# Zero matmuls in the places where TensorE is planned to stand

## The chip, the cores and the metric

The kernel runs on one core of a Trainium2 chip. The metric is device time in microseconds of one execution of the whole program; times are medians of several executions.

## What is computed

Two transformer-like blocks, one after the other, on a sequence of 256 tokens of width 2048, in float32. The first block has an "even" layer (a sparse attention with compressed, selected and windowed keys, called nsa; a differential attention; an attention to 256 memory rows) and an "odd" layer (an attention to the 64 best keys by an indexer, called dsa; memory attention again). The second block has two layers, each with four mixers side by side (retention, hgrn, mlstm, rwkv), an output projection, and a gated feed-forward net of width 5632.

```python
x = first_block(x, mem, ...)                 # even and odd layer
for l in range(DEPTH):                       # second_block, DEPTH = 2
    u = rms_norm_2(h, norm_pre_mix[l])
    p = (u @ w_in[l]).astype(jnp.float32)    # 2048 x 7952
    p_ret, p_hgrn, p_ml, p_rw = split_cols_2(p, GROUP_COLS)
    ...                                      # four mixers
    mixed = jnp.concatenate([o_ret, o_hgrn, o_ml, o_rw], axis=-1) @ w_out[l]
    h = h + rms_norm_2(mixed, norm_post_mix[l])
    u = rms_norm_2(h, norm_pre_ffn[l])
    ffn = (jax.nn.silu(u @ w_ffn_gate[l]) * (u @ w_ffn_up[l])) @ w_ffn_down[l]
    h = h + rms_norm_2(ffn, norm_post_ffn[l])
```

## The kernel before

Two kinds of work share TensorE. The **stream** is the projections. Their weights come in units of 256 rows by up to 512 columns. Each unit is split into a high part by ScalarE (line 514, two to four units ahead) and a low part by VectorE (line 527), and each product is three matmuls (high with high, low with high, high with low; line 621). A block of units is of kind `tokens` (two banks out of the first four, (0, 1) and (2, 3) in turn, moving rows of up to 512 weight columns), of kind `features` (up to four banks, 0 to 3 or 4 to 7, moving rows of 256 tokens), or of kind `plain` (line 600, f32). The activations that the stream multiplies have to be transposed first, by `turn` (line 738, transposes on line 745, then a high part by ScalarE and a low part by VectorE) or, at the first chunk after a norm, by `turn_first` (transposes on line 770).

The **lanes** are Python generators, one for each mixer or attention; they issue small f32 matmuls, transposes, and VectorE, ScalarE and GpSimd work in banks 4 to 7. A lane yields either nothing (due at once) or the semaphore marks that its next step will wait for.

The order of all engines' instructions is fixed when the program is built. Every engine has a planned clock (`pe.clock`, `dve.clock`, ...), every semaphore mark an expected time, and `expected_at` gives the latest of several. `weave` (line 434) picks the lane whose marks are due first, at time `at`, and asks `stream_first` (line 453) whether a chunk of the stream goes before it: it does when `at` is more than `SLACK` = 0.35 us behind the time at which the chunk can begin, when VectorE's or ScalarE's planned clock is 3.0 or 2.0 us ahead of it, or when TensorE's recent activity in the plan is below `ACTIVE`. Where no lane is due at all (`at` infinite: all wait for blocks of the stream), `fill(True)` transposes the next pieces and `step` runs a chunk. `fill` (line 545) waits for the finished mixer and calls `turn` itself. The planned cost of a VectorE operation is 0.16 us and 0.00104 us a column, whatever the operation (a reciprocal: six times as much a column).

A layer of the second block ends its output projection in `post_norm` (from line 1863 on): sums of squares by ScalarE (line 714, or 1825), a reduce and a power on VectorE and GpSimd (lines 723, 705, 706), then the update of the residual (line 1876), `turn_first`, and from there one `turn` after the other between chunks of the next projection.

Of the kernel before, what the change touches and what calls it, by code (L numbers as in the profile page):

```python
# [15 lines left out]
S = 256  # L16
# [4 lines left out]
UNIT = 2  # L21
# [4 lines left out]
DVE_LEAD, ACT_LEAD = 3.0, 2.0  # L26
PATIENCE = 0.1
WINDOW, ACTIVE = 3.4, 0.38
EPS = 1e-6
BIG = 1e30  # L30

# [99 lines left out]
def expected_at(marks):  # L131

    return max([expected.get((id(sem), value), 0.0) for sem, value in marks], default=0.0)
# [173 lines left out]
class Program:  # L307
# [3 lines left out]
    def build(self):  # L311
        nc = self.nc
        with ExitStack() as ctx:
            def sem(name):
                return ctx.enter_context(nc.semaphore(name))

            at = [(nc.sbuf_base + 31) // 32 * 32]
# [14 lines left out]
            self.low_split = Counter(sem("low_split"))  # L332
            self.unit_used = Counter(sem("unit_used"))
            self.bank_summed = Counter(sem("bank_summed"))
            self.first_loads = Counter(sem("ident_and_gains"), 16)
            self.mem_loaded = [Counter(sem(f"mem_loaded{i}"), 16) for i in range(4)]
            self.x_loaded = [Counter(sem(f"x_loaded{i}"), 16) for i in range(4)]
# [96 lines left out]
    def weave(self, *tasks):  # L434

        live = [[task, []] for task in tasks]
        while live:
            self.fill(False)
            self.lows()
            lane = min(live, key=lambda lane: self.due(lane[1]))  # L440
            at = self.due(lane[1])
            if at == math.inf:
                self.fill(True)
                assert self.step(), self.units[self.g][0].name
            elif self.stream_first(at):
                self.step()
            else:
                try:
                    lane[1] = next(lane[0])
                except StopIteration:  # L450
                    live.remove(lane)

    def stream_first(self, at):

        if self.g == len(self.units) or not self.can_run(*self.units[self.g]):
            return False
        blk, u = self.units[self.g]
        marks = [self.load_mark[self.g] if blk.kind == "plain" else self.low_mark[self.g]]
        if u + self.k == 0:
            marks += self.bank_free[blk.banks[self.n]]  # L460
        if blk.kind != "plain":
            marks += blk.AT.ready[blk.k0 + u * UNIT + self.k]
        begin = max(self.pe.clock, expected_at(marks))
        if begin < self.pe.clock + HOP and self.pe.activity() < ACTIVE:
            return True
        return (at > begin + SLACK or self.dve.clock > begin + DVE_LEAD or self.act.clock > begin + ACT_LEAD)
# [234 lines left out]

    def inv_rms(self, ss, n, eps=EPS):

        nc, dve, pool = self.nc, self.dve, self.pool
        pool.wait_ge(dve.did(nc.vector.tensor_scalar(ss, ss, 1.0 / n, eps, ALU.mult, ALU.add)))
        mark = pool.did(nc.gpsimd.tensor_tensor(ss, ss, self.minus_half[0:ss.shape[0], 0:ss.shape[1]], ALU.pow))  # L706
        dve.wait_ge(mark)
        return mark
# [305 lines left out]
    def first_turns(self):  # L1014

        nc, A, pe, act, dve, pool = self.nc, self.A, self.pe, self.act, self.dve, self.pool
# [52 lines left out]
        yield wanted  # L1069
        for q in (pe, act, dve):  # L1070
            q.wait_ge(*wanted, *[landed.now() for landed in self.x_loaded])
        for k in (1, 2):
            self.turn_rows(k, 4 + k)
            yield
# [1606 lines left out]
```

## Time and profile before

| | |
|---|---|
| time, median of 3 runs | 3916.73 us (3912.31 to 3918.07) |
| span of the profiled execution | 3913.3 us |
| TensorE busy | 3798.5 us (97%) |
| VectorE busy | 2256.0 us (58%) |
| ScalarE busy | 1795.6 us (46%) |
| mean granted clock of TensorE | 0.985 of full speed |
| chain that ended last | TensorE 88%, VectorE 6%, ScalarE 3% |

The span is from the first to the last instruction of one execution. TensorE is nearly always busy and nearly always at full clock, so what is left to see are the places where it stands or runs at the lower clock. In a timeline, a line gives the start, the duration of the merged instructions, engine, line of the kernel, operation, output and inputs, how many were merged, and in brackets how long the engine stood idle before them and who released it. An f32 matmul stands in the trace as two records, a fp32r matmul or a transpose as one.

### The profile page before, as it was taken

What the parts mean: (1) busy time and instruction counts of PE and PEld (TensorE: products, weight loads), DVE (VectorE), ACT (ScalarE), POOL (GpSimd) and SP (SyncE); (2) the same over time, 40 slices, a digit from 0 to 9 for tenths busy, and PEclk for the clock granted to TensorE, in tenths of its full rate; (3) what the DMA queues carried; (4) which work ended last, traced back from release to release, by engine and by line L of the source; (5) the groups of instructions that cost most, each with busy time, mean ns of one, the idle gap of its engine ahead of it and who ended that gap; (6) DMA issues with size and microseconds to landing.
All of it is one profiled execution on the core that took longest, in us unless ns stands there. A gap on an engine that the chain in (4) does not pass through costs nothing.

```text
span 3913.3 us, 49190 instructions
## 1 busy us (share of the span) xinstructions
PE 3798.5 (97%) x19948; PEld 3204.6 (82%) x19948; DVE 2256.0 (58%) x3532; ACT 1795.6 (46%) x2519; POOL 104.5 (3%) x61
## 2 busy tenths in 40 slices
PE   8999999999999999989999999999999989999998
PEld 7886778787898897778888888988987778888887
DVE  5665666675555746764454444566656664445444
ACT  6454545445454424544444444545325454444443
POOL 0000000000010000000000000010000000000000
PEclk9999999999999999999999999999999999999999
DMA  7655546563554405446666655544225446666654
GB/s 239 184 167 147 145 135 179 158 188 101 182 165 135 122 26 159 146 146 190 191 188 189 200 194 193 178 125 143 63 78 153 152 140 189 192 189 189 201 193 169
DMA packets 341426, 628.34 MB, mean 161 GB/s; under 512 B 21088, under 2 KB 63024, under 8 KB 340432
## 3 DMA queue, kind: packets, MB, share of 16 engines
q1 hardware_dynamic: 331920, 611.53, 51.7%
q10 hardware_dynamic: 9280, 13.69, 1.1%
q8 instruction: 156, 2.56, 0.3%
q14 instruction: 70, 0.57, 0.1%
HBM read 623.04 MB, written 2.10 MB: 160 GB/s over the span
## 4 chain that ended last, share of the span: by engine, by line
PE 88%; DVE 6%; ACT 3%; POOL 1%; issue 1%; DMA 1%; SPq 0%; ACTq 0%; DVEq 0%; POOLq 0%
PE bank L621 74%; DVE weights_low L527 2%; PE bank L745 1%; PE bank L1320 1%; PE bank L1417 1%; PE bank L2524 1%; PE bank L2538 1%; PE bank L2131 1%; PE bank L2537 1%; ACT weights_high L514 1%; PE bank L600 1%; PE bank L1400 1%; POOL stat L706 0%; PE bank L1323 0%; POOL arena L706 0%
## 5 line engine op out<-in xcount | busy, mean ns | idle before, releaser
L527 DVE TENSOR_TENSOR weights_low<-weights,weights_high 128x1024 fp32r<-128x1024 f32 (+3 forms) x1176 | 1393.7, 1195 | 979.0 <-ACT weights_high L514 967.7
L514 ACT ACTIVATE weights_high<-weights 128x1024 fp32r<-128x1024 f32 (+3 forms) x1176 | 1206.9, 1030 | 1341.2 <-PE bank L621 1284.1
L621 PE MATMUL bank<-weights_high,x_high 128*128 128x512 f32 (+3 forms) x2816 | 1116.7, 397 | 21.4 <-DVE weights_low L527 9.7
L621 PE MATMUL bank<-weights_low,x_high 128*128 128x512 f32 (+3 forms) x2816 | 1086.3, 386 | 0.0
L621 PE MATMUL bank<-weights_high,x_low 128*128 128x512 f32 (+3 forms) x2816 | 1086.0, 386 | 0.0
L621 PEld LDWEIGHTS bank<-weights_high,x_high 128*128 128x128 f32 x2816 | 536.0, 190 | 135.4 <-DVE weights_low L527 17.2
L621 PEld LDWEIGHTS bank<-weights_low,x_high 128*128 128x128 f32 x2816 | 535.0, 190 | 101.8
L621 PEld LDWEIGHTS bank<-weights_high,x_low 128*128 128x128 f32 x2816 | 536.3, 190 | 93.1
L621 PE MATMUL bank<-x_high,weights_high 128*128 128x256 f32 x960 | 279.6, 291 | 12.2 <-DVE arena L650 6.0
L621 PE MATMUL bank<-weights_high,y_high 128*128 128x512 f32 (+1 forms) x672 | 266.2, 396 | 8.7 <-DVE weights_low L527 6.5
L621 PE MATMUL bank<-weights_high,ff_high 128*128 128x512 f32 x704 | 274.0, 389 | 0.0
L621 PE MATMUL bank<-weights_low,ff_high 128*128 128x512 f32 x704 | 273.9, 389 | 0.0
L621 PE MATMUL bank<-weights_high,ff_low 128*128 128x512 f32 x704 | 273.9, 389 | 0.0
L621 PE MATMUL bank<-x_low,weights_high 128*128 128x256 f32 x960 | 273.1, 284 | 0.0
L621 PE MATMUL bank<-x_high,weights_low 128*128 128x256 f32 x960 | 273.0, 284 | 0.0
L621 PE MATMUL bank<-weights_low,y_high 128*128 128x512 f32 (+1 forms) x672 | 257.0, 382 | 0.0
L621 PE MATMUL bank<-weights_high,y_low 128*128 128x512 f32 (+1 forms) x672 | 256.7, 382 | 0.0
L621 PEld LDWEIGHTS bank<-x_high,weights_high 128*128 128x128 f32 x960 | 185.4, 193 | 19.1 <-DVE weights_low L527 12.8
L621 PEld LDWEIGHTS bank<-x_low,weights_high 128*128 128x128 f32 x960 | 185.6, 193 | 1.0 <-issue 1.0
L621 PEld LDWEIGHTS bank<-x_high,weights_low 128*128 128x128 f32 x960 | 185.5, 193 | 0.0
L621 PEld LDWEIGHTS bank<-weights_low,ff_high 128*128 128x128 f32 x704 | 132.1, 188 | 27.5
L621 PEld LDWEIGHTS bank<-weights_high,ff_high 128*128 128x128 f32 x704 | 132.1, 188 | 27.5
(385 smaller groups left out, 3618.8 us busy)
## 6 DMA issues: line engine op xcount, KB each, us to landing
weights<-in_w_in_dram SPq DMA_DIRECT2D x208, 512.0 KB, 3.6
weights<-in_w_ffn_gate_dram SPq DMA_DIRECT2D x176, 512.0 KB, 3.7
weights<-in_w_ffn_up_dram SPq DMA_DIRECT2D x176, 512.0 KB, 3.6
weights<-in_w_ffn_down_dram SPq DMA_DIRECT2D x176, 512.0 KB, 3.6
weights<-in_w_out_dram SPq DMA_DIRECT2D x128, 512.0 KB, 3.6
weights<-in_even_w_in_dram SPq DMA_DIRECT2D x88, 512.0 KB, 3.6
weights<-in_odd_w_in_dram SPq DMA_DIRECT2D x80, 512.0 KB, 3.6
weights<-in_mem_w_kv_dram SPq DMA_DIRECT2D x32, 512.0 KB, 4.2
```

The lines of the kernel that those rows point to most:

```text
L514: self.high_mark[g] = self.high_split.count(act.ran(nc.scalar.activation(high, raw, ACT.Copy)), act.clock)
L527: self.low_mark[g] = self.low_split.count(dve.ran(nc.vector.tensor_tensor(low, raw, high.bitcast(F32), ALU.subtract)), dve.clock)
L600: ins = pe.ran(nc.tensor.matmul(bank[0:R2, 0:CMP_HID], blk.AT[:, k, :, :].rearrange("p g c -> p (g c)"), wv[:, l, :], start=(k == 0), stop ...
L621: ins = pe.ran(nc.tensor.matmul(out, l, r, start=(u + c + x + y == 0), stop=(u == blk.n - 1 and c == UNIT - 1 and y == 1)))
L745: ins = pe.ran(nc.tensor.transpose(ps[:, (j * T + t) * P:(j * T + t + 1) * P], src(c + j, t), self.c("ident")))
L1320: ins = pe.ran(nc.tensor.matmul(s["ps"], u["qT"], u["kT"], start=True, stop=True))
L1400: ins = pe.ran(nc.tensor.transpose(bank[0:w, c * P:(c + 1) * P], s["e"][:, c * P:c * P + w], self.c("ident")))
L1417: ins = pe.ran(nc.tensor.matmul(o, s["eT_buf"][:, c * P:(c + 1) * P], u["v"][c], start=(c == 0), stop=(c == kt - 1)))
L2131: ins = pe.ran(nc.tensor.matmul(self.ps[b][:, i * P:(i + 1) * P], k3[h, c, t * P:(t + 1) * P], q3[h, c, t * P:(t + 1) * P], start=True, st ...
L2524: ins = pe.ran(nc.tensor.matmul(self.ps[b][:, i * P:(i + 1) * P], M4[n][:, 0:P], TT[n][:, 0:P], start=True, stop=True))
L2537: pe.ran(nc.tensor.matmul(self.ps[b][:, i * S:i * S + P], TT[n][:, P:2 * P], Y[n], start=True, stop=True))
L2538: ins = pe.ran(nc.tensor.matmul(self.ps[b][:, i * S + P:(i + 1) * S], Y[n], TT[n][:, P:2 * P], start=True, stop=True))
```

## The change

A method `keep_busy` is added and is called from `weave` before a stream chunk (with the time at which the chunk can begin, from the new method `begins`, which repeats the working of `stream_first`) and before a lane's step (with the earlier of that time and `at`). If the plan has TensorE standing until then for at least 0.9 us (recent planned activity below 0.6) or 2.0 us (otherwise), and one of banks 0 to 3 is neither in use by the block under way nor still waiting for its evacuation in the plan, then f32 matmuls of the identity with a 128x256 table of zeros are put in, as long as more than 0.9 us are left, for at most 8 us. They carry no semaphore. The branch of `weave` for `at` infinite does not call it. It is switched on once the parameters have landed, near the end of the first task.

```diff
+FILL_LEAST, FILL_LONG, FILL_MOST, FILL_ACTIVE = 0.9, 2.0, 8.0, 0.6
...
             elif self.stream_first(at):
+                self.keep_busy(self.begins())
                 self.step()
             else:
+                self.keep_busy(min(at, self.begins()))
                 try:
                     lane[1] = next(lane[0])
...
+    def keep_busy(self, until):
+
+        pe = self.pe
+        until = min(until, pe.clock + FILL_MOST)
+        if not self.filling or until < pe.clock + (FILL_LEAST if pe.activity() < FILL_ACTIVE else FILL_LONG):
+            return
+        taken = ()
+        if self.g < len(self.units):
+            blk, u = self.units[self.g]
+            taken = blk.banks if u + self.n + self.k else ()
+        for b in (3, 2, 1, 0):
+            if b not in taken and expected_at(self.bank_free[b]) < pe.clock:
+                break
+        else:
+            return
+        pe.wait_ge(*self.bank_free[b])
+        while until > pe.clock + FILL_LEAST:
+            pe.ran(self.nc.tensor.matmul(self.ps[b][:, 0:S], self.c("ident"), self.c("zeros"), start=True, stop=True))
+
+    def begins(self):
+
+        if self.g == len(self.units) or not self.can_run(*self.units[self.g]):
+            return math.inf
+        blk, u = self.units[self.g]
+        marks = [self.load_mark[self.g] if blk.kind == "plain" else self.low_mark[self.g]]
+        if u + self.k == 0:
+            marks += self.bank_free[blk.banks[self.n]]
+        if blk.kind != "plain":
+            marks += blk.AT.ready[blk.k0 + u * UNIT + self.k]
+        return max(self.pe.clock, expected_at(marks))
...
             q.wait_ge(*wanted, *[landed.now() for landed in self.x_loaded])
+        self.filling = True
```

## Rows read from the trace of the kernel before

**Rows 1.** Spans and mean granted clock of the cores.
```profile
core 0: 3913.3 us, clock 0.985
```

**Rows 2.** Busy time in chosen stretches; columns are named in the first line.
```profile
core 0: us, PE busy (x) PEld busy (x) DVE busy (x) ACT busy (x) POOL busy (x), PEclk, DMA share, GB/s
...
940.00:954.00 14.00, 5.87 (x23) 4.50 (x21) 6.94 (x13) 6.31 (x12) 1.64 (x1) 0.63 0.11 38
...
1485.00:1498.00 13.00, 8.33 (x26) 6.47 (x25) 10.18 (x9) 4.22 (x7) 1.88 (x1) 0.74 0.35 104
...
1720.00:1735.00 15.00, 7.73 (x29) 5.93 (x29) 10.86 (x20) 4.64 (x13) 0.70 (x1) 0.66 0.20 61
2463.00:2474.00 11.00, 6.20 (x32) 5.65 (x32) 8.37 (x16) 4.38 (x10) 0.70 (x1) 0.69 0.21 66
...
2705.00:2725.00 20.00, 17.66 (x130) 15.60 (x128) 15.60 (x29) 13.44 (x25) 0.00 (x0) 1.00 0.56 162
2747.00:2765.00 18.00, 14.59 (x66) 14.41 (x65) 11.03 (x18) 6.53 (x9) 0.00 (x0) 0.62 0.18 49
2898.00:2918.00 20.00, 20.00 (x82) 18.79 (x81) 6.22 (x8) 5.03 (x8) 0.88 (x1) 0.57 0.34 104
...
3159.00:3175.00 16.00, 8.73 (x30) 6.67 (x30) 11.01 (x20) 5.04 (x14) 0.70 (x1) 0.68 0.24 77
```

**Rows 3.** Timeline of TensorE: the five stalls that the plan can see.
```profile
948.02 1.09 PE L745 MATMUL bank<-const,arena 128*128 128x128 f32 x4 [7.77 <-DVE arena L1148]
...
1490.58 0.79 PE L621 MATMUL bank<-weights_high,x_high 128*128 128x512 f32 x1 [4.67 <-DVE weights_low L527]
...
1725.52 1.12 PE L770 MATMUL bank<-const,x_residual 128*128 128x128 f32 x4 [5.46 <-DVE x_residual L1876]
...
2467.23 1.11 PE L770 MATMUL bank<-const,x_residual 128*128 128x128 f32 x4 [4.05 <-DVE x_residual L1876]
...
3164.67 1.12 PE L770 MATMUL bank<-const,x_residual 128*128 128x128 f32 x4 [5.46 <-DVE x_residual L1876]
```

**Rows 4.** Timeline of TensorE: stalls that it can't fill.
```profile
1694.62 1.08 PE L745 MATMUL bank<-const,arena 128*128 128x128 f32 x4 [1.94 <-DVE x_low L750]
...
2712.89 0.36 PE L621 MATMUL bank<-x_high,weights_high 128*128 128x256 f32 x1 [2.34 <-DVE arena L650]
...
2750.95 0.63 PE L621 MATMUL bank<-weights_high,x_high 128*128 128x348 f32 x1 [3.41 <-DVE arena L650]
...
3132.41 1.12 PE L745 MATMUL bank<-const,arena 128*128 128x128 f32 x4 [5.76 <-DVE arena L1950]
```

**Rows 5.** Timeline of TensorE: the stream at the lower and at the full clock.
```profile
1491.60 0.63 PE L621 MATMUL bank<-weights_low,x_high 128*128 128x512 f32 x1
1492.03 0.63 PE L621 MATMUL bank<-weights_high,x_high 128*128 128x512 f32 x1
...
1497.43 0.39 PE L621 MATMUL bank<-weights_low,x_high 128*128 128x512 f32 x1
1497.66 0.39 PE L621 MATMUL bank<-weights_high,x_high 128*128 128x512 f32 x1
```

**Rows 6.** Timeline of TensorE behind `turn_first`, in layer 0.
```profile
1727.38 0.76 PE L621 MATMUL bank<-weights_high,x_high 128*128 128x512 f32 x1 [0.75 <-DVE x_low L778]
...
1732.47 1.47 PE L745 MATMUL bank<-const,x_residual 128*128 128x128 f32 x12
...
1735.00 0.47 PE L621 MATMUL bank<-weights_high,x_high 128*128 128x512 f32 x1 [1.06 <-DVE x_low L757]
```

**Rows 7.** Timeline of VectorE in the same place.
```profile
1730.90 1.22 DVE L527 TENSOR_TENSOR weights_low<-weights,weights_high 128x1024 fp32r<-128x1024 f32 x1
1733.98 0.88 DVE L757 SCALAR_TENSOR_TENSOR x_low<-bank,param_cols,x_high 128x256 fp32r<-128x256 f32 x2 [1.87 <-ACT x_high L753]
```

**Rows 8.** Timeline of TensorE: a further transpose behind the first stall.
```profile
952.23 1.11 PE L745 MATMUL bank<-const,arena 128*128 128x128 f32 x4 [0.36 <-DVE y_low L750]
```

**Rows 9.** Timeline of TensorE: f32 matmuls of 256 columns in a row.
```profile
309.76 3.64 PE L600 MATMUL bank<-weights,arena 128*30 128x256 f32 x16 [0.46 <-ACT arena L964]
```

**Rows 10.** Timeline of VectorE: an operation that the plan prices by its columns.
```profile
2540.15 0.68 DVE L2077 TENSOR_SCALAR arena<-arena 128x1024 f32<-128x1024 f32 x1
```

More of the change, by code:

```diff
@@ L334, in build @@
             self.bank_summed = Counter(sem("bank_summed"))
+            self.filling = False
             self.first_loads = Counter(sem("ident_and_gains"), 16)
```

## The prediction

> **What bounds the kernel now.** TensorE does: it is busy for 97% of the span, and the chain that ended last is 88% its work. I first read the mean granted clock, 0.985 of full speed over 3913.3 us [rows 1]. The missing 0.015 are 58.7 us of clock, so the lower of the two levels (1.2 instead of 2.4 GHz) held for some 117 us. Then I cut the span into short stretches and looked for those with a clock below 1.00. There are fourteen before the last 10 us; [rows 2] has the seven that matter most, and one stretch (2705 to 2725) that kept 1.00. In the timeline of TensorE I read what stood ahead of each [rows 3, 4]. Three kinds are to be seen. In most, the engine had stood for some microseconds, and at its return ran at half pace: fp32r matmuls of 512 columns start 0.43 us apart at 1492 and 0.23 us apart at 1497 [rows 5]. In the stretch 2898 to 2918 it never stood (busy 20.00 of 20.00 us) and had a clock of 0.57 all the same, during small f32 matmuls [rows 2]. And in 2705 to 2725 it stood for 2.34 us between full streams and the clock stayed at 1.00 [rows 2, 4].
>
> The change doesn't shorten a stall, since what ends one is VectorE's or ScalarE's work. It can only keep the clock up for the work behind it. So the gain is counted in that work alone.
>
> **Which stalls get zeros.** The method acts where neither a lane nor the stream is due in the plan. I went through the code at each stall.
> - 940 to 948, 7.77 us [rows 3]: the memory lane yields the marks of its norm (line 1148), the stream's activations aren't transposed. The lane's due time is what the method sees. Filled.
> - 1486 to 1490, 4.67 us: the low split stands behind rwkv's last norm on VectorE. The block starts in banks 2 and 3, long free. Filled, once the plan is at that chunk.
> - 1720, 2463 and 3159, of 5.46, 4.05 and 5.46 us: `post_norm` yields the mark of the residual's first update; the stream can't run. Filled, since the pair of banks that the last block didn't use is free.
> - 2750, 3.41 us [rows 4]: a features block has filled banks 0 to 3 and none is evacuated. The search for a bank finds none. Not filled; the same holds for the 2.34 us at 2712.
> - 1694 and 3132, 1.94 and 5.76 us [rows 4]: the waits are inside `fill` and `turn`, reached with all lanes waiting for blocks (the branch without the call) or behind steps that are due at once. Not filled. Two more stalls behind `turn`, near 517 and 3033, are alike.
> - 2898 to 2918 has no stall and nothing to fill.
>
> So five of the fourteen stretches change.
>
> **What each is worth.** Half pace costs half of the time spent at it.
> - 1486: half pace from 1490.58 [rows 3] until shortly before 1497.43 [rows 5], by the clock of the stretch (13.00 us at 0.74, so 3.4 us of clock, of which TensorE was idle for a small part) [rows 2]. About 6.1 us of stream at half pace, 3.0 us lost. The zeros end at most 0.9 us ahead of the release in the plan, and fp32r matmuls follow at once: all 3.0 us come back.
> - 1720: the four transposes of `turn_first` took 1.12 us [rows 3]; four elsewhere take about 0.65 us at full clock (the 12 of line 745 at 1732 took 1.47 us [rows 6]), so 0.45 us. The stream then ran at half pace from 1727.38 to about 1732.2 [rows 6], 2.4 us lost. Not all of that returns: the transposes behind it need ScalarE, and the low part (line 757) VectorE, which is at a split (line 527) until 1732.12 [rows 7]. Line 757 began at 1733.98 and can begin at about 1732.1 to 1732.3, so what follows the wait at 1735.00 [rows 6] moves by at most 1.9 us, the 0.45 us within it. I take 1.9.
> - 3159 is the same place of the other layer, with the same 5.46 and 1.12 us: 1.9.
> - 2463: 0.45 us in the transposes, and half pace until about 2472.8 in a stretch of 11.00 us at 0.69 (3.4 us of clock, part of it in the stall) [rows 2]. Features matmuls, 24 to the first unit, give VectorE more time. Between 1.5 and 2.5; I take 2.1.
> - 940: 0.45 us in the first transposes. Behind them are three hops between TensorE, ScalarE and VectorE before the stream resumes after the transposes of 952.23 [rows 8], so half pace counts only in part. Between 0.4 and 2; I take 1.0.
>
> Together 3.0 + 1.9 + 1.9 + 2.1 + 1.0 = 9.9 us.
>
> **What the zeros cost.** The nearest row is a run of f32 matmuls of 256 columns: 16 records, eight matmuls, in 3.64 us [rows 9]. Less the tail of the last one, that is 0.435 us a matmul. The loop stops with 0.9 us or less to go, and so the last one ends at least 0.46 us before the planned end. At a stall of the planned length they cost nothing; the cover is the stall itself. Filling the five takes 16 + 9 + 11 + 8 + 11, about 55 matmuls or 110 records, and adds some 24 us to TensorE's busy time. No wait is new on the chip, since the bank's evacuation is long done, and SP, ScalarE, VectorE and GpSimd get no instruction. Where the plan sees a stall and the chip has none, each costs 0.435 us, with the whole stream behind it. The trace of before can't show how many there are. The lower bound is nothing. For the upper one, the plan prices a VectorE operation by its columns: 0.16 + 0.00104 x 1024 = 1.22 us for line 2077, which took 0.68 us [rows 10]. A few such in a row move planned releases a microsecond or two late. They stand in hgrn, where banks 0 to 3 are mostly held by features blocks. I take three matmuls, 1.3 us. The new planned clock also lets `fill` and `lows` act earlier, which reorders work by a step here and there; that can be a gain or a loss of a few us, and I leave it at 0.
>
> **The sum.** 3913.3 - 9.9 + 1.3 = 3904.7 us of span. The median of the runs is 3.4 us above the profiled span, so the time is 3908.1, or 3908, which is 0.22% less.
>
> **The rivals.**
> - *The clock falls all the same* (rival A). Behind the zeros of four of the five stalls there is a rest: up to 0.9 us of standing, four transposes, and 0.75 us of standing again [rows 6]. At 1694 a similar piece, four transposes and a wait of 1.94 us, ended in transposes that took 1.08 us, half pace again [rows 4]. For it: the transposes may do little for the clock. Against it: 2.34 us of standing between full streams went by at 1.00. Then the split-wait at 1486 keeps its 3.0 us, each of the three `post_norm` places keeps only the 0.45 us and one of them the rest (1.35 + 1.5), 940 nothing: 5.9 - 1.3 = 4.6 us, so 3912. The Trainium skill, on the page "TensorE: Matmul & The Clock Gate", Part 4, says that transposes don't count as activity for the clock in the way that matmuls do. The trace doesn't decide it; by that rule rival A is the likelier one for the four places, and 3912 the time.
> - *The change does little of what it says* (rival B): the planned stalls are shorter than 2.0 us while the stream's activity is above 0.6, or no bank is free. Against it, the planned prices fit the measured ones for most operations. 3917.
> - *Zeros where the chip has no stall* (rival C), slower than before. In mixers and attentions planned activity is low and 0.9 us of planned standing is enough. The gain of 9.9 us is used up by 23 zero matmuls that find no stall; 60 of them cost 26 us, less 9.9, so 3933; 35 make it 3922. For it: the plan knows no half clock, and a plan that is wrong by a microsecond is enough. Against it: TensorE stands for 114 us in all, in stalls that a plan of this kind would see much alike.
> - *More is cured* (rival D): the reordering and added activity also lift some of the other nine stretches; at 3.0 us each, three of them give 3899.
>
> **How the numbers follow.** The forecast has 0.42, rival A 0.20, B 0.05, C 0.19, D 0.14. A measurement of this kernel can tell about 0.2% from no change, 7.8 us, so the border is 3908.9, close to the forecast; I give 0.25 of its 0.42 to the faster side and 0.17 to within. Faster: 0.25 + 0.14 = 0.39. Within: 0.17 + 0.20 + 0.05 + 0.02 of C = 0.44. Slower: 0.17. The range goes from D's 3899 to 3924, a little beyond C with 35 idle matmuls, and leaves out C's tail and a little below D.
>
> **What would show it.** A new group of f32 matmuls from `const` into a bank, about 110 records for the five places, and more than 200 if rival C holds. At the line 770 transposes: 0.65 instead of 1.12 us. A mean clock near 0.99; if it stays at 0.985, rival A or B. In the stall of line 527 near 1486, half pace gone. The waits of 5.46 us for line 1876 replaced by one below 1 us. The stretches near 2750 and 2898 unchanged. I'm wrong if those five places keep their clock and the time doesn't move, or if the zeros stand where nothing stood.

## The result, and the profile after

| | before | after |
|---|---|---|
| time, median | 3913.82 us (20 runs, 3908.25 to 3920.85) | 3925.43 us (20 runs, 3908.86 to 3935.63) |
| ratio | | 1.0025 (95% interval 1.0015 to 1.0035) |
| span of the profiled execution | 3913.3 us | 3907.2 us |
| its mean granted clock | 0.985 | 0.990 |
| TensorE busy, records | 3798.5 us, 19948 | 3828.7 us, 20164 |

The kernel became 0.25% slower. I had forecast 3908 us, 0.22% less, in a range from 3899 to 3924. The time went up instead of down and ended outside the range. Two things stand out beside the ratio. The time after spreads over 27 us where before it spreads over 13. And the profiled execution of after is among the shortest of its program: it is 6 us shorter than that of before, while the medians say 12 us longer. Whoever reads that one trace alone would call the change a gain.

The page of after, its engines and its chain, and then, from the groups of TensorE by form (busy us, mean ns of one), the one that is new. Line numbers of after are 35 or 36 higher than before's behind the new methods (621 became 656, 527 became 562, 770 became 805).

```profile
PE 3828.7 (98%) x20164; PEld 3233.1 (83%) x20164; DVE 2256.2 (58%) x3532; ACT 1794.6 (46%) x2519; POOL 101.8 (3%) x61
...
PE 91%; DVE 5%; ACT 2%; issue 1%; DMA 1%; POOL 1%; SPq 0%; ACTq 0%; DVEq 0%; POOLq 0%
```

```profile
L474 PE MATMUL bank<-const 128*128 128x256 f32 x216 | 49.3, 379 | 0.0
```

VectorE and ScalarE are as busy as before. TensorE has 216 records more, which are 108 zero matmuls, not the 55 of my working. Set side by side, the two programs have the same order of instructions on VectorE and ScalarE, and TensorE's differs in the zeros alone, which stand in 16 places. So nothing was reordered, and that term of the sum was rightly 0.

The same work as in the stretches of [rows 2], as it ran in after (it starts up to 12 us earlier there): around the five stalls that I meant, and, in the fifth and sixth rows, the work that before ran at half pace behind the stall of 2750 and near 2898.

```profile
core 0: us, PE busy (x) PEld busy (x) DVE busy (x) ACT busy (x) POOL busy (x), PEclk, DMA share, GB/s
940.00:954.00 14.00, 12.66 (x64) 10.38 (x64) 7.59 (x14) 6.87 (x12) 1.64 (x1) 1.00 0.13 38
1482.00:1495.00 13.00, 13.00 (x61) 11.04 (x60) 11.71 (x10) 4.43 (x8) 1.15 (x1) 1.00 0.45 136
1713.00:1728.00 15.00, 13.39 (x67) 10.75 (x66) 12.29 (x24) 7.08 (x19) 0.70 (x1) 1.00 0.31 98
2454.00:2465.00 11.00, 10.31 (x66) 8.87 (x65) 8.79 (x17) 5.68 (x14) 0.70 (x1) 1.00 0.22 72
2737.00:2755.00 18.00, 14.59 (x73) 14.41 (x72) 12.25 (x18) 6.32 (x9) 0.00 (x0) 0.72 0.24 62
2892.00:2912.00 20.00, 20.00 (x144) 18.25 (x144) 6.49 (x10) 5.52 (x11) 0.00 (x0) 1.00 0.38 111
3156.00:3172.00 16.00, 14.38 (x71) 11.31 (x70) 13.30 (x25) 8.08 (x22) 0.70 (x1) 1.00 0.28 81
```

The clock column is the thing to see: 0.63, 0.74, 0.66, 0.69 and 0.68 at the five stalls before, 1.00 now. Behind the unfilled stall of 2750 half pace stayed (0.62 before, 0.72 now). Near 2898 it is gone in this execution, though no zero stands there; that will come back below. The timeline of TensorE at three of them answers to [rows 3 and 6]; the first, the 1486 and the 1720 stall.

```profile
940.04 7.50 PE L474 MATMUL bank<-const 128*128 128x256 f32 x34
947.98 0.63 PE L780 MATMUL bank<-const,arena 128*128 128x128 f32 x4 [0.44 <-DVE arena L1184]
...
1482.03 5.34 PE L474 MATMUL bank<-const 128*128 128x256 f32 x24
1487.02 0.58 PE L656 MATMUL bank<-weights_high,x_high 128*128 128x512 f32 x1
...
1713.56 5.77 PE L474 MATMUL bank<-const 128*128 128x256 f32 x26
1719.18 0.66 PE L805 MATMUL bank<-const,x_residual 128*128 128x128 f32 x4
1719.67 0.60 PE L474 MATMUL bank<-const 128*128 128x256 f32 x2
1720.79 0.47 PE L656 MATMUL bank<-weights_high,x_high 128*128 128x512 f32 x1 [0.52 <-DVE x_low L813]
```

The waits of 7.77 and 5.46 us are filled, four transposes of line 805 take 0.66 instead of 1.12 us, and there is even one zero matmul between them and the first chunk. At 1486 there is no wait at all: the zeros fill it to the last, which will matter.

Now the same view at two of the other places, after and then before.

```profile
1331.56 3.62 PE L474 MATMUL bank<-const 128*128 128x256 f32 x16
1334.82 0.51 PE L656 MATMUL bank<-weights_high,x_high 128*128 128x348 f32 x1
...
2757.25 2.32 PE L474 MATMUL bank<-const 128*128 128x256 f32 x10
2759.22 0.51 PE L656 MATMUL bank<-weights_high,x_high 128*128 128x348 f32 x1
```

```profile
1334.21 0.32 PE L621 MATMUL bank<-weights_low,x_high 128*128 128x348 f32 x1
1335.60 0.43 PE L621 MATMUL bank<-weights_high,x_high 128*128 128x348 f32 x1 [1.06 <-DVE weights_low L527]
...
2765.77 0.32 PE L621 MATMUL bank<-weights_low,x_high 128*128 128x348 f32 x1
2765.93 0.32 PE L621 MATMUL bank<-weights_high,x_high 128*128 128x348 f32 x1
```

Eight zero matmuls stand where TensorE had waited 1.06 us, and five where it hadn't waited at all in this trace (1.07 us in a second trace of before, in which no half pace came behind 2750). In the kernel's own plan these stalls had 4.11 and 3.00 us. All places, with the stall in the plan, which comes out when the program is built:

| place (us of after) | plan's stall | zero matmuls | their time at 0.435 us | stall in the trace of before |
|---|---|---|---|---|
| 209 | 2.32 | 4 | 1.7 | 1.63 |
| 411 | 2.47 | 4 | 1.7 | 0.61 |
| 819 | 2.96 | 5 | 2.2 | 1.11 |
| 1051 | 2.62 | 4 | 1.7 | 0.91 |
| 1331 | 4.11 | 8 | 3.5 | 1.06 |
| 2633 | 0.95 | 1 | 0.4 | 0 |
| 2757 | 3.00 | 5 | 2.2 | 0 |
| 2916 | 4.96 | 10 | 4.4 | 1.51 |
| sum of these without 209 | | 37 | 16.1 | 5.2 |
| 940 | 8.0 | 17 | 7.4 | 7.77 |
| 1482 | 5.74 | 12 | 5.2 | 4.67 |
| 1713 | 6.28 | 13 + 1 | 6.1 | 5.46 |
| 2454 | 4.59 | 9 + 1 | 4.4 | 4.05 |
| 3156 | 6.28 | 13 + 1 | 6.1 | 5.46 |

The "+ 1" is a zero matmul behind `turn_first`, for a planned stall of 1.03 us. At the five stalls, too, the plan is longer than the chip, by 0.2 to 1.1 us. I call 940, 1713, 2454 and 3156 **the four** (by the times of before: 940, 1720, 2463, 3159; 52 zero matmuls without the three behind `turn_first`), 1482 by its old name **1486**, and the upper eight places **the others** (41).

**Where the time went.** I cut both traces into stretches of 1 us, up to 13 us before the end of the span (the last stretch has no stream). A span is then four things: 13 us and some 3749 us of work at full clock (3745 to 3752 in the traces of this case), the time in which TensorE stands, the zeros at 0.435 us, and the *half-pace loss*, which is (1 - clock) x busy time summed over the stretches.

| profiled execution of | span | stands | zeros | both | half-pace loss |
|---|---|---|---|---|---|
| before | 3913.3 | 104.5 | 0 | 104.5 | 46.6 |
| after | 3907.2 | 68.2 | 47.0 | 115.2 | 31.8 |
| after, run again (first experiment) | 3923.1 | 67.0 | 47.0 | 114.0 | 49.8 |
| after, third time | 3924.5 | 68.7 | 47.0 | 115.7 | 51.2 |
| before, run again | 3916.5 | 104.9 | 0 | 104.9 | 51.7 |

Standing plus zeros is nearly the same in all three traces of after (114.0 to 115.7), and 10.3 us (on average) above before. That is the net cost of the zeros in time at which TensorE does nothing useful. The half-pace loss isn't a property of the program: it is 31.8 in one execution of after and 51.2 in another. The next sections take the two apart.

### The profile page after: what moved, and what is told of

Same layout as the page of the kernel before. It is cut to its first block, busy times and chain, and to the rows that moved or that the text cites. A ratio compares the mean times of both kernels' runs of the same rounds, so it can differ in the third digit from the quotient of the medians.

```text
span 3907.2 us, 49620 instructions
## 1 busy us (share of the span) xinstructions
PE 3828.7 (98%) x20164; PEld 3233.1 (83%) x20164; DVE 2256.2 (58%) x3532; ACT 1794.6 (46%) x2519; POOL 101.8 (3%) x61
## 4 chain that ended last, share of the span: by engine, by line
PE 91%; DVE 5%; ACT 2%; issue 1%; DMA 1%; POOL 1%; SPq 0%; ACTq 0%; DVEq 0%; POOLq 0%
PE bank L656 76%; DVE weights_low L562 2%; PE bank L780 1%; PE bank L1356 1%; PE bank L1453 1%; PE bank L2560 1%; PE bank L2167 1%; PE bank L2574 1%; PE bank L2573 1%; PE bank L474 1%; ACT weights_high L549 1%; PE bank L635 1%; PE bank L1436 1%; PE bank L1359 0%; POOL stat L741 0%
## 5 line engine op out<-in xcount | busy, mean ns | idle before, releaser
L656 PEld LDWEIGHTS bank<-x_high,weights_high 128*128 128x128 f32 x960 | 185.7, 193 | 16.3 <-DVE weights_low L562 10.2
```

What stands on the lines that cost most here:

```text
L656: ins = pe.ran(nc.tensor.matmul(out, l, r, start=(u + c + x + y == 0), stop=(u == blk.n - 1 and c == UNIT - 1 and y == 1)))
```

## The experiments

Each kernel was timed beside the kernel before on the same chip; the groups of kernels ran on different chips, and the mean of before was 3912.8 to 3917.2 us on them. Where two kernels of different chips are compared, the difference of each to its own before is the safer number. Means are given beside medians, because the runs of one program differ by up to 28 us.

### The same two kernels again

```diff
(no edit)
```

> The changed kernel once more, for a second trace of it and the clock of each run. Theory 1 (the zeros outlast the stalls and the clock that they save is lost again elsewhere): about 11 us longer than the kernel before at the same mean clock, a mean clock of 0.985 to 0.988 in most runs, so 3918 to 3930, and the trace shows other or longer stretches at half pace than in the first one, in the rwkv mixers (near 1400 and 2830). Theory 2 (the change saves clock and the slow runs are a disturbance of the chip): most runs near 3909 with 0.990. The order of the other engines' instructions is the same as before, so reordering is out.

> The kernel before once more, for a second trace and the clock of each of its runs. Theory 1: runs of 3908 to 3921 whose length goes with the mean clock (0.001 of clock for 3.9 us), and the same lowered stretches behind stalls, with the stretches in the rwkv mixers (1408 and 2898) longer or shorter. Theory 2: all runs within 2 us of each other at 0.985.

> The changed kernel a third time, for a trace. All theories: idle time plus the time of the 108 zeros 10 to 14 us above the idle time before; the rest of the length is the half pace in the rwkv mixers (near 1400, 1480, 2835, 2905), 0 to 10 us at each, another in each run. Theory 2: a run of over 3925 has half pace near 1480 and no stall left behind the zeros there.

After again: 3920.08 us (12 runs, 3905.61 to 3928.36), ratio 1.001 (0.9996 to 1.0023). Before again: 3912.41 us (11 runs, 3907.03 to 3918.11), 0.9995 (0.9987 to 1.0004). After a third time: one run, 3925.99. All 33 runs of after together have a mean of 3921.8 us, against 3914.4 of before (147 runs). So after is slower by 0.1 to 0.25%. The second measurement, 1.001, lies outside the interval of the first, 1.0015 to 1.0035, and taken alone it isn't told from no change. Theory 1 holds as far as it goes: a mean clock of 0.988, and the added half pace lies in rwkv.

Where the three traces of after differ is in four stretches of the rwkv mixers. The same stretches, in the first trace of after and then in the second:

```profile
1395.00:1430.00 35.00, 35.00 (x228) 30.01 (x224) 14.78 (x30) 10.43 (x19) 1.90 (x1) 1.00 0.24 62
1466.00:1491.00 25.00, 25.00 (x144) 22.70 (x143) 13.76 (x16) 9.44 (x15) 2.90 (x1) 1.00 0.48 147
2818.00:2858.00 40.00, 40.00 (x204) 34.12 (x203) 12.83 (x28) 9.50 (x18) 1.90 (x1) 0.74 0.18 45
2880.00:2920.00 40.00, 40.00 (x286) 37.04 (x285) 18.53 (x28) 12.91 (x22) 2.90 (x1) 1.00 0.34 105
```

```profile
1395.00:1430.00 35.00, 35.00 (x160) 30.23 (x159) 9.97 (x21) 8.46 (x16) 1.90 (x1) 0.71 0.18 51
1466.00:1491.00 25.00, 25.00 (x140) 23.03 (x139) 6.14 (x13) 4.11 (x9) 0.00 (x0) 0.70 0.21 67
2818.00:2858.00 40.00, 40.00 (x255) 36.55 (x256) 11.61 (x22) 8.07 (x16) 1.90 (x1) 0.79 0.06 18
2880.00:2920.00 40.00, 40.00 (x336) 38.01 (x334) 18.31 (x30) 8.75 (x16) 0.00 (x0) 1.00 0.09 27
```

TensorE is busy for all of these stretches, and the same program ran two of them at full clock in one execution and at about 0.7 in the next. It is the kind of stretch that [rows 2] showed at 2898 to 2918: small f32 matmuls of 64 columns between a few of the stream. Its half-pace loss over the four stretches:

| kernel | near 1410 | 1475 | 2835 | 2900 | sum |
|---|---|---|---|---|---|
| before / again | 3.4 / 3.4 | 0 / 0 | 0 / 5.1 | 8.5 / 8.5 | 11.9 / 17.0 |
| after | 0 | 0 | 10.2 | 0 | 10.2 |
| after again | 10.2 | 8.5 | 10.2 | 0 | 28.9 |
| after third | 10.2 | 0 | 10.2 | 8.5 | 28.9 |

Rwkv alone makes 19 us of difference between two traces of after, which is most of its spread and the reason why its profiled execution was short.

### Long and short stalls

```diff
+        if until < pe.clock + 3.5:
+            return
```

That is the kernel with the long stalls; the one with the short stalls has `until >= pe.clock + 3.5`.

> Zeros only where the plan has a stall of 3.5 us or more. The five stalls of the prediction keep theirs, and 1331 and 2916 perhaps; those of 411, 819, 1051, 2757 and the single ones go. Theory 1: 3 to 6 us less than the changed kernel, since zeros that outlast their stall go. If the rise is due to the long fills (activity without a pause), it stays at 3925. Theory 2: no difference to the changed kernel, within 2 us.

> The complement: zeros only where the plan has a stall below 3.5 us. Theory 1: slower than the kernel before by the time by which these zeros outlast their stalls, 3 to 8 us, at a clock as before, 0.985. Theory 2: as the kernel before within 2 us. If only these carry the loss, 3921 to 3925.

Long stalls alone (82 zeros): 3914.1 us, 1.0003 (0.9993 to 1.0013). Short ones alone (26 zeros): 3927.07, 1.0035 (1.0023 to 1.0047). Zeros in places whose planned stall is below 3.5 us bring a loss in the sum; their trace stands and fills for 109.3 us against 104.5. (Three of them are the single ones behind `turn_first`. At 1720 and 2463 this trace gains 1.2 and 0.8 us on before with these alone, where traces without any zeros there are level with before or up to 0.3 us behind it.) The loss, 13 us in the mean, is larger than the 3 to 8 us that I had expected; standing and zeros are 4.8 of it, and its trace has 8.4 us more half-pace loss than that of before, all of it in rwkv. The long ones gain nothing in the mean (their trace stands and fills for 110.3 us), though five of the seven places are the five stalls. The other two, 1331 and 2916, are of the misplanned kind.

### The five, the four, and the others

```diff
+        if self.g == len(self.units) or until < pe.clock + 3.5 or self.units[self.g][0].name not in ("o.out_dsa0", "0.rtq", "0.gate0", "1.hgq", "1.gate0"):
+            return
```

The names are those of the next block at 940, 1486, 1720, 2463 and 3159. The four leaves "0.rtq" (1486) out. The others returns where the name is one of the five, and has no condition on the length.

> Zeros only at the five stalls of the prediction (940, 1486, 1720, 2463, 3159; one block each). Theory 1 (zeros cost where the chip's stall is shorter than the plan's, and those were the other places; the clock saved at the five is real): faster than the kernel before by 6 to 9 us, 3905 to 3908. Theory 2 (zeros at the stall of 1486 also take away its slack: TensorE that comes late through half pace in rwkv is no longer caught up there): mean gain 4 to 7 us, and the runs spread wider than those of the kernel before, over more than 16 us. Theory 3 (a clock saved at a stall is lost again elsewhere): the mean clock stays at 0.985 and the time at 3914 or above.

> The same without 1486, so only at stalls that begin with TensorE's own last matmul and end a fixed time after it. Theory 1: 3 us slower than with five, gain 4 to 6 us. Theory 2: as fast as with five or faster, gain 5 to 8 us, and a spread no wider than that of the kernel before (16 us). Theory 3: no gain.

> Zeros at all places of the change but these five: 51 matmuls less the single ones, where the stall waits for VectorE's split or an evacuation and was 0 to 1.6 us long. Theory 1 and 2: slower than the kernel before by 10 to 14 us, 3924 to 3928; idle time plus zeros (0.435 us each) about 11 us more than the idle time of the kernel before; in theory 2 a spread above 20 us. Theory 3: slower by the same, at a lower mean clock than before, 0.980.

| | median | ratio | mean | stands + zeros | half-pace loss |
|---|---|---|---|---|---|
| five | 3911.34 | 0.9992 (0.998 to 1.0005) | 3910.0 | 106.9 | 34.8 |
| four | 3906.47 | 0.9978 (0.9967 to 0.9988) | 3904.5 | 103.6 | 25.1 |
| others | 3928.57 | 1.0039 (1.0026 to 1.0052) | 3928.1 | 113.2 | 47.9 |

The four beat both kernels: 8 us below before. The others lose 15 us, of which 8.7 are standing plus zeros (113.2 - 104.5). This settles the sign: the loss is that of the other places. Adding 1486 to the four costs 5.4 us in the mean (95% interval about 0 to 11, by the spread of the 12 runs each), where I had counted a gain of 3.0. The five gained 2.8 us where theory 1 had 6 to 9 and theory 2 had 4 to 7, and they spread over 26 us, as theory 2 had it.

To see each place by itself, I compared the start of one and the same instruction in two traces. The *lead* is its start in a kernel less its start in before; the change of the lead over a place is what the place gained (negative) or lost. At 940 it goes from -0.1 to -2.0 in after.

| place | my estimate | after, again, third | the four | others alone |
|---|---|---|---|---|
| 940 | -1.0 | -1.9, -2.0, -1.9 | -1.9 | 0 |
| 1486 | -3.0 | -2.7, -2.7, -2.6 | -5.2 (no zeros there) | -4.9 (no zeros there) |
| 1720 | -1.9 | -2.5, -2.5, -2.5 | -2.4 | 0 |
| 2463 | -2.1 | -1.7, -1.7, -1.7 | -1.7 | 0 |
| 3159 | -1.9 | -3.2, -3.1, -3.1 | -3.1 | 0 |
| 209 | 0 | 0, 0, 0 | 0 | 0 |
| 411, 819, 1051 | 0 | +2.3, +2.2, +2.1 | 0 | +2.3 |
| 1331 | 0 | +2.1, +2.1, +2.1 | 0 | +3.6 |
| 2757 | 0 | +1.3, +1.3, +1.3 | 0 | -3.5 |
| 2916 | 0 | +1.9, +2.0, +2.3 | +3.2 (no zeros there) | +2.0 |

At the four places after gains 9.3 us (6.9 forecast), and the kernel with the four alone has a mean 8.3 us below that of before on its chip. With zeros these gains, taken against the one trace of before, are the same in every trace to 0.1 us. Without zeros the half pace behind a stall varies from trace to trace: at 3159 the second trace of before is 1.0 us ahead of the first, and two others without zeros there 1.5, so the gain at that place is nearer 2.3 us in the mean than 3.1. Before, run again, also lost 1.5 us at 1331 and gained 4.3 at 2757 without a zero. The row of 2916 has the end of rwkv's half pace in it.

### 1486: a stall that is also slack

> Zeros only at the stall of 1486 (12 of them, 5.3 us). Theory 2 (the stall is slack for what rwkv's half pace ahead of it delayed): mean gain between -3 and +2 us, a gain of 2.4 us where the clock was full ahead of the stall and a loss of 3 us where it was not; spread wider than that of the kernel before. The prediction's view (3.0 us come back at a cost of nothing): 3 us faster in the mean, spread as before.

The edit is that of the five with "0.rtq" as the only name. It gave 3913.78 us, 1.0003 (0.9993 to 1.0013), though its zeros keep the clock: over the place its lead falls by 2.6. The traces say why. TensorE's timeline there, in the kernel with the four:

```profile
1484.07 0.32 PE L658 MATMUL bank<-weights_low,x_high 128*128 128x344 f32 x1
1486.73 0.50 PE L658 MATMUL bank<-weights_high,x_high 128*128 128x512 f32 x1 [2.34 <-DVE weights_low L564]
1487.07 0.39 PE L658 MATMUL bank<-weights_high,x_low 128*128 128x512 f32 x1
```

and in after again, where the zeros are:

```profile
1498.21 5.34 PE L474 MATMUL bank<-const 128*128 128x256 f32 x24
1503.20 0.58 PE L656 MATMUL bank<-weights_high,x_high 128*128 128x512 f32 x1
```

The stretch just ahead, near 1475, is one of the four of rwkv. Where it runs at full clock (before in both traces), the stall is 4.67 us and half pace follows [rows 3, 5]. Where it runs at half pace (the four in both traces, the others), TensorE comes to the stall 7.4 us later. VectorE's split waits for other work that comes only 5.1 to 5.3 us later, so the stall is only 2.34, 2.48 and 2.65 us. Half pace doesn't follow it (0.50 us, then 0.23 between starts), and the place gives back 5.2, 5.0 and 4.9 us. With zeros it gives 2.6 or 2.7 in every trace, whether half pace was ahead or not, since their number is fixed when the program is built. So filling it gains 2.7 us when the rwkv stretch was fast and loses 2.5 when it was slow. The gain can be smaller: in three of the seven traces with a fast stretch and no zeros here, half pace held for half as long behind the stall, and filling would have brought back 1.3 us less. Slow and fast are about equally frequent (half pace near 1475 in 8 of the 17 traces, of all kernels but the one of the thin matmuls below), and the sum is about nothing, as this kernel measured: its mean is 0.8 us above that of before.

The stall of 1.51 us at 2916 is its mirror: in before, half pace stood ahead of it (8.5 us) and left 1.51; in the four it was full clock ahead, and the stall was 3.83 us.

### What one zero costs

```diff
             pe.ran(self.nc.tensor.matmul(self.ps[b][:, 0:S], self.c("ident"), self.c("zeros"), start=True, stop=True))
+            (self.nc.tensor.matmul(self.ps[b][:, 0:S], self.c("ident"), self.c("zeros"), start=True, stop=True))
```

> As r7, each zero matmul issued twice (88 instead of 44). Theory 1 (what outlasts a stall is on the path, and is priced by its number): 44 x 0.435 = 19 us more than r7, so 3945 to 3949, less only what stall was left. If the cost of r7 were an overhead of breaking the stream and not the zeros' own time, it would rise by a few us only, to 3930.

The zeros of the others, each issued twice (82 instead of 41). Their own time in the traces went from 19.1 to 36.8 us: 17.7 more for 41 more matmuls, 0.43 each, as priced. Standing plus zeros went from 113.2 to 132.0 us. The 18.8 more include 2.0 us of stall at 1486, which was longer here because rwkv near 1475 ran at full clock. The time was not as expected: mean 3931.4 us (4 runs), only 3.3 above the others alone and not 17 to 21 (1.7 by the differences to before; the two ran on different chips). In the traces 9.3 us of it came back as half pace that was absent, 38.6 us against 47.9; why there was less isn't shown. So the price of a zero is sure, and the sum of a program's time still isn't.

### The thin matmuls of rwkv

```diff
                     pe.wait_ge(*self.bank_free[b])
+                    nc.tensor.matmul(self.ps[b][:, 0:S], self.c("ident"), self.c("zeros"), start=True, stop=True)
                     for x in range(2):
```

The added line stands at both loops over `e` in rwkv's recurrence.

> As r6 (four stalls), and one zero matmul more in front of each of the 32 groups of thin f32 matmuls (64 columns) in the last part of rwkv, 8 in each of the four stretches near 1400, 1480, 2835 and 2905, where TensorE never stands. Theory 4 (thin matmuls lower the clock, no stall is needed, and this makes the runs differ): the half pace in these stretches goes or shrinks (0 to 29 us, some 15 in the mean), the cost is 14 us, so the mean is 3900 to 3906 and the spread falls from 18 to below 10 us. Rival (the clock there has another cause): half pace as before, 14 us slower than r6, 3918 to 3920, spread as in r6.

The four, and one zero matmul ahead of each of 32 groups of the thin matmuls: 3910.45 us, 0.9984 (0.9975 to 0.9992), in a range of 11 us instead of 18. The four stretches:

```profile
1395.00:1430.00 35.00, 35.00 (x225) 29.44 (x223) 14.22 (x30) 9.62 (x18) 1.90 (x1) 1.00 0.20 53
1466.00:1490.00 24.00, 24.00 (x164) 22.07 (x163) 7.33 (x11) 7.47 (x13) 1.24 (x1) 1.00 0.38 115
2818.00:2858.00 40.00, 40.00 (x263) 34.29 (x263) 16.48 (x35) 11.34 (x21) 1.90 (x1) 1.00 0.18 47
2880.00:2920.00 40.00, 39.23 (x279) 35.96 (x278) 15.27 (x25) 11.58 (x21) 2.90 (x1) 1.00 0.30 91
```

All are at 1.00 now, which none of the other 17 traces has, and the mean clock of its 12 runs is 0.9927, the highest of all kernels. So what TensorE executes in them decides, and no stall is needed. The 32 matmuls cost 14 us by their price and bring back most of it: against before on its own chip the kernel gains 5.7 us, where the four gain 8.3 and, a second time, 10.7. Its mean, 3908.6, is above the 3900 to 3906 of my theory 4, and the spread, 11 us, is just above the 10 that I had set.

### The five zeros at 2757

```diff
+        here = self.g < len(self.units) and self.units[self.g][0].name == "1.mlv0" and self.units[self.g][1] == 4
+        if not here and (self.g == len(self.units) or until < pe.clock + 3.5 or self.units[self.g][0].name not in ("o.out_dsa0", "0.gate0", "1.hgq", "1.gate0")):
+            return
```

That is the four with the five zeros at 2757; a second kernel has three more behind them. The opposite edit takes them out of after (`return` where the next block is "1.mlv0"). They test whether zeros ahead of a rwkv stretch decide how much half pace it has, by moving the moment at which its thin matmuls begin.

> r6 plus the five zeros of one place of the change, in the middle of the block behind the stall of 2750 (2.2 us, no stall on the chip). Theory 5 (these zeros move rwkv's thin matmuls near 2830 to where they meet the clock badly, after the half pace of 2743 to 2754 that ends at the same instant in every run): half pace of about 10 us near 2830 in nearly every run, so 2.2 + 5 to 8 = 7 to 10 us slower than r6, 3911 to 3915. Rival (chance of the run alone): 2.2 us slower than r6, 3907.

> The same with eight zeros there, 3.5 us. Theory 5: the place of the thin matmuls is shifted further, half pace near 2830 is back to 0 or small, so only 3.5 us slower than r6 and faster than r12 though it has more zeros, 3907 to 3909. Rival (more zeros cost more, or zeros there lower the clock by themselves): at least as slow as r12.

> The changed kernel without these five zeros. Theory 5: 7 to 10 us faster than the changed kernel (mean of its 33 runs 3921.8), 3912 to 3915, and no half pace near 2830. Rival: 2.2 us faster, 3919 to 3920.

> The kernel with zeros in the four stalls and, five of them, at 2757, a second time, beside the four alone on the same chip. Read from the first pair: 3899.5 mean with the five at 2757 against 3904.5 without. If the five are worth nothing or gain, this comes out at or below the other one of this call (ratio to before 0.995 to 0.998). If they cost what idle and zeros say, 2.2 us, it is 2 us above it. If they cost 9 us, as leaving them out of the changed kernel said (3921.8 mean against 3912.7), it is 9 us above it, near 3913.

> Zeros in the four stalls alone (940, 1720, 2463, 3159), a second time: 0.9978 of the kernel before the first time, so 8 us below it again, if the gain belongs to the edit; within 3 us of it, if the first was one chip's way of placing the half pace of the thin matmuls.

| | median | ratio | mean | rwkv, sum of its four stretches |
|---|---|---|---|---|
| four + 2757 | 3899.96 (5 runs) | 0.9955 (0.9943 to 0.9967) | 3899.5 | 8.5 |
| the same again | 3902.94 (12) | 0.9976 (0.9962 to 0.9989) | 3904.7 | 27.2 |
| four again | 3900.72 (7) | 0.9973 (0.996 to 0.9987) | 3903.2 | 20.5 |
| four + 8 there | 3909.18 (11) | 0.9984 (0.9974 to 0.9994) | 3911.0 | 15.3 |
| after less 2757 | 3913.57 (12) | 0.999 (0.998 to 1.0001) | 3912.7 | 13.6 |

The first of them is by its median the fastest kernel of all and speaks against my theory 5, by which the five cost 7 to 10 us; measured again, on another chip, it is level with the four. The traces speak against theory 5 too. Near 2830 it wanted some 10 us of half pace with five zeros, and nothing or little with eight or none. The two kernels with five have 0 there, the one with eight 8.5, after without them 5.1. Only the time of after without them, 3912.7, is as it said. All 17 runs with the five have a mean of 3903.2 us, all 19 without, 3904.0 (11.7 and 9.2 below the means of before on their chips). Added to the four they cost nothing that can be seen, and the four's gain holds. Taken out of after, they bring 9 us (3921.8 to 3912.7; 12 by the differences to before on each chip), though they take only 2.2 us and standing plus zeros hardly went down (114.5, from 114.0 to 115.7). So what else is in the program decides. That half pace lies differently is all that the traces show; why it lies worse in after is open.

## Why the prediction was wrong, by its steps

**The five stalls, right.** All five got zeros and kept the clock. The gains by place sum to 12.0 us where I had 9.9: 940 and 1720 were undersized (1.9 for 1.0, 2.5 for 1.9), 2463 oversized (1.7 for 2.1). At 3159, 3.2 came back for 1.9 against the trace that I had read, and about 2.3 against the traces without zeros there taken together. So the sum is nearer 11 than 12. The part that I took off at 1720 for VectorE's split was too large.

**Rival A, refuted.** Behind the zeros came 0 to 0.44 us of standing, four transposes and, before the stream went on, waits of at most 0.52 us, and the clock stayed 1.00 there in every trace of after. At three of the four places another zero matmul stood behind the four transposes, which I hadn't counted on; at 940 there was none, and the clock stayed as well. By the Trainium skill's rule on transposes ("TensorE: Matmul & The Clock Gate", Part 4) I had made this rival the likelier one at these places; the time that I derived from it, 3912, didn't come. The longest row of transposes behind the zeros is twelve in 1.5 us, at 940, so nothing tests the rule in a longer one.

**The unfilled stalls, right for those I named, incomplete in the rest.** 2750 kept its 3.41 us, 1694 its 1.94 and 3132 its 5.76 in every trace, without zeros. But I looked for zeros only where the trace of before had a stall. Rival B (the change does little) and rival D (more is cured by reordering) are out as well: 67 zeros stand at the five stalls, and no order changed.

**The cost of zeros, the step that failed.** "The trace of before can't show how many there are ... I take three matmuls, 1.3 us." There were 41 outside the five stalls. Four of them, at 209, found a stall of their own length and cost nothing; the other 37 stand in places with stalls of 0 to 1.5 us. (At the five themselves there are 67 where I had 55, since the plan's stalls are longer than those that I took from the trace.) Standing plus zeros rose by 10.3 us, eight times my term. The mechanism was that of rival C, at a net size of some 24 matmuls (10.3 us by 0.435), just above my 23, and to it I gave 0.19. I had evidence against my three: [rows 10] showed the plan pricing a 0.68 us operation at 1.22, and "a microsecond or two late" over some seven releases is 10 us. Which of the plan's prices makes it wrong at these eight places no run shows. I took "They stand in hgrn, where banks 0 to 3 are mostly held" for cover, without counting which blocks begin there in free banks. The clause "Against it: TensorE stands for 114 us in all" was no argument: most of that is at places where the zeros weren't.

**1486, right in its size and wrong in its worth.** Its 3.0 us were measured as 2.7 in every trace. But in "At a stall of the planned length they cost nothing" the stall's length was taken from one trace. In others TensorE arrives 7.4 us later, and the stall takes up 2.0 to 2.3 of them. Zeros of fixed number remove that. In the mean the term is about 0 by the kernel with 1486 alone, or by the difference of the five and the four +5.4, with 0 at the edge of its interval.

**Half pace without a stall, not in the sum.** I wrote of 2898 to 2918 that it "has no stall and nothing to fill" and left it unchanged. It and three stretches like it are worth between 0 and 29 us in one execution. The two traces of before have 12 and 17 in them; the three of after, 10, 29 and 29. An estimate for the mean of after's runs: its mean time, less 13 us at the end of the span and some 1.5 between span and time, less 3746 us of work and 115 of standing and zeros, leaves 46 us of half pace; 21 to 22 of it lie outside rwkv in its three traces, so about 25 inside. For before the same working gives 47 and 35, so about 12. That is 13 us more; the traces themselves, three against two, have 8 more.

**The sum again.** By the four parts of a span: standing plus zeros +10.3, half-pace loss outside rwkv -13 (34.7 in both traces of before, 21 to 22 in those of after), half pace in rwkv +13, and the work at full clock 2 less in the traces. That is +8, and the means say +7 over all chips and +10 in the first measurement. The first two terms rest on rows that repeat from trace to trace. The third is what the means leave over, so the sum has to close and doesn't prove it, and its error is a few us. So what stopped the gain is shown in two pieces of unequal strength: the 10.3 us of zeros and standing are measured, and the rest is rwkv's half pace, inferred. That the zeros shift it is made likely by two kernels (the others lose 15 us of which 8.7 are their own; after less 2757 gains 9 for 2.2), and the doubled others speak against a rule, since they lost hardly more. How they shift it is open.

## What to carry to other kernels

Filler work is worth it in the stalls that a trace shows and that are long in every trace; a plan can see stalls of 2.5 to 5 us where the chip has 0 to 1.5, and each filler that outlasts its stall is paid in full by the engine that bounds. Before a stall is filled or shortened, ask what it absorbs: one that ends on another engine's clock is slack for everything late ahead of it. And where the clock of one and the same stretch differs from one execution to the next, one profiled execution says little about a few us: compare means of ten or more runs, and compare standing, fillers and half pace in the traces apart.

## What the hardware showed

- TensorE's granted clock was at 0.57 to 0.79 over 20 to 40 us in which its records leave no gap, in small f32 matmuls of 64 columns between fp32r ones of the stream, and in the same instructions at 1.00 in another execution. One f32 matmul of 256 columns ahead of each group held it at 1.00. The Trainium skill ("TensorE: Matmul & The Clock Gate", Part 1, "What's actually happening") says that the clock's watch runs on by itself and isn't started anew with the kernel, so that the same kernel has more or fewer slow matmuls at its start. The spread of one program's rwkv stretches, 10.2 against 28.9 us, would fit that in the middle of a kernel, but no run here tests it. That page explains the slow clock by standing, long or in short pieces, and here the trace shows none. The ends of matmuls are modelled in it, so it can't tell whether the array rests between these small ones.
- A stall of 2.34 us between full streams kept the clock in before, near 2712 [rows 2, 4], and the same 2.34 us were followed by half pace in after (a clock of 0.93 over 2690 to 2715). The 3.41 us at 2750, the same to 0.01 us in all 18 traces, had half pace behind them in 12. Whether a stall of 2 to 3 us costs anything isn't fixed.
- A zero matmul of 256 columns in f32 costs 0.43 to 0.44 us at full clock (17 of them in 7.50 us, 12 in 5.34), and four transposes right behind them took 0.63 to 0.66, against 1.09 to 1.12 at half pace.
